# Two of the four weight sums of each FFN pair made by accumulating DMAs instead of VectorE

## The reference

```
h = rms_norm(x, ffn_norm_w)                                   # 256 x 2048
a = silu(h @ w_ffn_gate) * (h @ w_ffn_up)                     # both 2048 x 5632
x = x + a @ w_ffn_down                                        # 5632 x 2048
```

## Time and profile before

| | before |
|---|---|
| median of 3 runs | 2090.38 us (2086.85 to 2092.23) |
| the profiled execution | 2089.39 us |
| its span in the trace | 2087.7 us |
| TensorE busy | 2079.0 us |
| VectorE busy | 1372.1 us, 66% |
| ScalarE busy | 1072.2 us, 51% |
| GpSimd busy | 144.5 us, 7% |
| mean granted TensorE clock | 0.999 of full speed |

### The profile page before, as it was taken

How to read it: one execution, slowest core, us unless ns; L and a number is a source line. 1 busy time by engine, 2 the same in 40 slices (tenths; PEclk the granted TensorE clock), 3 DMA queues, 4 the chain that set the end, 5 groups by cost and what they waited for, 6 DMA issues and landing times.

```text
span 2087.7 us, 28374 instructions
## 1 busy us (share of the span) xinstructions
PE 2079.0 (100%) x9658; PEld 1715.0 (82%) x9658; DVE 1372.1 (66%) x1677; ACT 1072.2 (51%) x1380; POOL 144.5 (7%) x174
## 2 busy tenths in 40 slices
PE   9999999999999999999999999999999999999999
PEld 7888877778888888888888888888888888888887
DVE  6676456665767777777664555577777887764443
ACT  5444455554566666666654444455555555543333
POOL 1121000000012222222000000000000000000000
PEclk9999999999999999999999999999999999999999
DMA  7656665554565555555575555556656666566554
GB/s 237 205 177 209 197 198 169 163 176 138 189 204 172 189 186 185 183 182 181 171 231 193 191 189 187 189 176 197 201 161 198 205 199 202 161 223 205 199 200 141
DMA packets 207541, 394.46 MB, mean 189 GB/s; under 512 B 15665, under 2 KB 21218, under 8 KB 207218
## 3 DMA queue, kind: packets, MB, share of 16 engines
q1 hardware_dynamic: 204530, 384.79, 56.7%
q0 software_dynamic: 2336, 8.46, 1.3%
q10 hardware_dynamic: 608, 0.34, 0.1%
HBM read 387.18 MB, written 2.16 MB: 186 GB/s over the span
## 4 chain that ended last, share of the span: by engine, by line
PE 93%; DVE 3%; issue 2%; DMA 1%; ACT 1%; DVEq 0%; SPq 0%; ACTq 0%
PE acc L1500 84%; PE side L1516 3%; PE side L1870 2%; DVE w_raw L1311 1%; PE side L1743 1%; DVE w_lo L1306 1%; PE acc L1870 1%; PE side L1598 1%; ACT w_hi L784 1%; DMA w_raw<-in_w_in 0%; DMA x_row<-in_x 0%; PE side L1749 0%; PE acc L1516 0%; PE side L1672 0%; DVE w_lo L847 0%
## 5 line engine op out<-in xcount | busy, mean ns | idle before, releaser
L847 DVE TENSOR_TENSOR w_lo<-w_raw,w_hi 128x1024 fp32r<-128x1024 f32 x536 | 668.2, 1257 | 538.0 <-ACT w_hi L463 537.1
L463 ACT ACTIVATE w_hi<-w_raw 128x1024 fp32r<-128x1024 f32 x536 | 564.0, 1058 | 708.0 <-PE acc L1500 651.9
L1500 PE MATMUL acc<-w_hi,h_hi 128*128 128x512 f32 x1280 | 511.4, 400 | 0.1
L1500 PE MATMUL acc<-w_hi,h_lo 128*128 128x512 f32 x1280 | 499.9, 391 | 0.0
L1500 PE MATMUL acc<-w_lo,h_hi 128*128 128x512 f32 x1280 | 498.8, 390 | 0.0
L784 ACT ACTIVATE w_hi<-w_raw 128x1024 fp32r<-128x1024 f32 x209 | 220.2, 1060 | 211.5 <-PE acc L1500 120.9
L1306 DVE TENSOR_TENSOR w_lo<-w_raw,w_hi 128x1024 fp32r<-128x1024 f32 x209 | 252.6, 1223 | 96.1 <-ACT w_hi L784 89.9
L1500 PEld LDWEIGHTS acc<-w_hi,h_hi 128*128 128x128 f32 x1280 | 240.7, 188 | 52.5 <-issue 5.5
L1500 PEld LDWEIGHTS acc<-w_hi,h_lo 128*128 128x128 f32 x1280 | 240.5, 188 | 51.5
L1500 PEld LDWEIGHTS acc<-w_lo,h_hi 128*128 128x128 f32 x1280 | 241.0, 188 | 49.3 <-issue 1.9
L1500 PE MATMUL acc<-w_hi,x2T_hi 128*128 128x512 f32 x528 | 206.7, 391 | 0.1
(11 more groups left out here) (276 smaller groups left out, 2352.2 us busy)
## 6 DMA issues: line engine op xcount, KB each, us to landing
w_raw<-in_w_in SPq DMA_DIRECT2D x320, 512.0 KB, 4.2
w_raw<-in_w_ffn_gate SPq DMA_DIRECT2D x88, 512.0 KB, 3.7
w_raw<-in_w_ffn_up SPq DMA_DIRECT2D x88, 512.0 KB, 4.5
w_raw<-in_w_ffn_down SPq DMA_DIRECT2D x88, 512.0 KB, 3.5
w_raw<-in_w_ssm_proj SPq DMA_DIRECT2D x64, 512.0 KB, 4.2
w_raw<-in_w_attn_proj SPq DMA_DIRECT2D x32, 512.0 KB, 3.5
w_raw<-in_w_out SPq DMA_DIRECT2D x32, 512.0 KB, 3.5
acs_b<-acs_scratch POOLq DMA_DIRECT2D x16, 512.0 KB, 7.1
```

The source lines that it names most:

```text
L463: nc.scalar.activation(w_hi[:, r], w_raw[:, r], ACT.Copy).then_inc(hi_ready, 1)
L847: nc.vector.tensor_tensor(w_lo[:, r], w_raw[:, r], w_hi[:, r].bitcast(F32), ALU.subtract).then_inc(lo_ready, 1)
L1500: done = nc.tensor.matmul(acc[p][:, t], a[:, k0 + kk, cut], w[:, r, kk], start=first and kk == n == 0, stop=last and kk == UK - 1 and n == 2)
```

## The change

The first sum and the slot 1 sum are no longer VectorE instructions. GpSimd issues for each pair two DMAs that read one slot and add it to another in place. The first waits until the remainder of P1 is done (it overwrites slot 0) and slot 1 is loaded; the second waits until the first has landed (it overwrites slot 1, which the first reads) and slot 2 is loaded. Ahead of each DMA stands a multiply of two elements a partition on GpSimd. ScalarE's roundings of P5 and P7 wait for the DMAs' semaphores, and VectorE waits for the second DMA before the slot 2 sum, which keeps its place in VectorE's order.

```diff
+PLAIN_UNITS = UPC * (7 * D // CW + 2 * G) + 3 * UPC * D // CW
...
-        weights_summed, p1_ready, mids_free, gates_summed = (...)
+        first_summed, third_summed, weights_summed, p1_ready, mids_free, gates_summed = (...)
...
@@ scalar engine, operand_hi
                     if n < 3:
                         act.wait_ge(raw_in[source], raw.now(RAWS // 2) * (16 // RING) + 16)
+                    elif n == 4:
+                        act.wait_ge(third_summed, i * 16 + 16)
+                    elif n == 3:
+                        act.wait_ge(first_summed, i * 16 + 16)
                     else:
-                        act.wait_ge(weights_summed, i * 4 + (n - 2))
+                        act.wait_ge(weights_summed, i * 2 + (n - 4))
...
@@ vector engine, ffn_pair
-                    if at == FIRST7 - LEAD:
-
-                        dve.wait_ge(raw_in[1], raw.now(RAWS // 2) * (16 // RING) + 16)
-                        weights_sum(0, 0, 1)
                     if at == FIRST7 - LEAD + 2:
-                        weights_sum(1, 1, 2)
-                        dve.wait_ge(weights_summed, i * 4 + 2)
+
+                        dve.wait_ge(third_summed, i * 16 + 16)
                         weights_sum(2, 0, 2)
                     if at == FIRST7 - LEAD + 3:
-                        dve.wait_ge(weights_summed, i * 4 + 3)
+                        dve.wait_ge(weights_summed, i * 2 + 1)
                         weights_sum(3, 2, 3)
...
@@ gpsimd, behind everything it did before
+            def third_weights_sum(i):
+
+                pool.wait_ge(pool_step, own.now())
+                pool.wait_ge(lo_ready, i * OPERANDS + (PLAIN_UNITS + FIRST7 + 1))
+                pool.wait_ge(raw_in[1], i * (16 // RING * RAWS) + (16 // RING * (PLAIN_UNITS + RAWS // 2) + 16))
+                nc.gpsimd.tensor_tensor(y_scratch, y_ss, y_ss, ALU.mult).then_inc(pool_step, 1)
+                own.step()
+                pool.dma_start(w_raw[:, 0], w_raw[:, 1], accum_op=ALU.add).then_inc(first_summed, 16)
+                pool.wait_ge(pool_step, own.now())
+                pool.wait_ge(first_summed, i * 16 + 16)
+                pool.wait_ge(raw_in[2], i * (16 // RING * RAWS) + (16 // RING * (PLAIN_UNITS + RAWS // 2) + 16))
+                nc.gpsimd.tensor_tensor(y_scratch, y_ss, y_ss, ALU.mult).then_inc(pool_step, 1)
+                own.step()
+                pool.dma_start(w_raw[:, 1], w_raw[:, 2], accum_op=ALU.add).then_inc(third_summed, 16)
+
+            third_weights_sum(0)
+            with repeat(pool, FF // CW - 1, [(own, 2)]) as i:
+                third_weights_sum(i + 1)
```

More of the change, by code:

```diff
@@ L310, in layer @@
         s_summed, s_hi_ready, s_lo_ready = sem("s_summed"), sem("s_hi_ready"), sem("s_lo_ready")
-        weights_summed, p1_ready, mids_free, gates_summed = (sem(n) for n in ("weights_summed", "p1_ready", "mids_free", "gates_summed"))
+        first_summed, third_summed, weights_summed, p1_ready, mids_free, gates_summed = (sem(n) for n in ("first_summed", "third_summed", "weights_summed", "p1_ready", "mids_free", "gates_summed"))
         gate_f_ready, a_ready, a_T, a_hi_ready, a_lo_ready = (sem(n) for n in (
```

## The result

| | before | after |
|---|---|---|
| median | 2090.08 us | 2137.64 us |
| profiled execution's span | 2087.7 us | 2135.9 us |

The change makes the kernel slower: the ratio is 1.0229, 95% interval 1.0214 to 1.0243, 47.6 us. The forecast of 2168 us had the direction and the place; it was 30 us too high.

A forecast was written before the change was run, and what follows sets the result against it. TensorE was taken to bound the kernel. Delays of P5's remainder (68 us), the clock (9) and the first pair (2) added 79 us to 2089.4, giving 2168 us; own range 2146 to 2203, 8 in 10 within 2112 to 2245.

The forecast's parts named there:

- What bounds, and the most to be won: TensorE bounds; taking work from VectorE wins only TensorE's waits for remainders, 5.5 us in all 11 pairs.
- A delay of P5's remainder is one of TensorE, whole: At P5 in each pair, TensorE has no slack and loses the same time; forecast 6.2 us a pair, 68 us.
- The link: One of two chained steps per pair: GpSimd's wake-up, multiply and DMA; x = L + 0.35 us.
- L: Time from an accumulating DMA's issue to its landing, taken as 6.0 us; a pair's delay is 2L - 5.8 us.
- So I start from 4.2: Step sizing the landing from GpSimd's best 512 KB load, 4.2 us, as nothing else is in flight there.
- The surcharge for accumulating: Added to the plain landing: 1.44 us for reading 512 KB more, and something for the addition, reaching 6.0 us.
- the addition and second read cost almost nothing: Rival: landing 4.0 to 5 us, pairs 2.2 to 4.2 us later, kernel 2115 to 2146 us; chance 0.17.
- The clock: After TensorE's idle 5.4 us ahead of P5, lower clock loses 1.65 us, 0.8 uncovered a pair, 9 us in all.
- the rival of short landings: Rival with landings of 4.0 to 5 us, idle times too short for the clock to fall each time; chance 0.17.
- The slow accumulation: Rival: accumulating DMAs land in above 7.6 us; at 8.8 the kernel takes 2230 us; chance 0.23.
- the clock staying low for most of a pair: Rival: TensorE stays at 1.2 GHz for most of a pair; 2190 us and up; chance 0.03.
- Both DMAs hidden: Rival: landings below 2.9 us leave P5 ready early; at 2.6 the stall goes, 2084 us; chance 0.03.

The follow-up runs named there:

- c4_two_sums_out: The kernel before with the first and the slot 1 sum left out and no DMA in their place: 2083.74 us, ratio 0.9972.
- b1_copy: The changed kernel with both DMAs copying instead of adding: 2095.10 us, ratio 1.0032 to the kernel before.
- b2_half: The changed kernel with each accumulating DMA adding only the first 512 of its slot's 1024 columns: 2100.88 us, ratio 1.0059 to the kernel before.
- d1_together: The changed kernel with the first DMA adding slot 2 instead of slot 1, so both DMAs are in flight at once: 2105.48 us, ratio 1.0080 to before.
- c1_fill: The changed kernel with ten more matmuls a pair on TensorE ahead of P5, filling its idle time: 2129.28 us, ratio 1.0193 to the kernel before.
- e1_p5_ahead_fill: The changed kernel with the second DMA's wait and slot 2 sum behind P5's remainder, plus ten matmuls a pair ahead of P7: 2119.97 us, ratio 1.0146 to before.
- b3: The changed kernel with only the first sum made by a DMA, the slot 1 sum back on VectorE: 2091.67 us, ratio 1.0011 to before.
- b4: The changed kernel with only the slot 1 sum made by a DMA, the first sum back on VectorE: 2087.45 us, ratio 0.9994 to before.
- c3_p5_ahead: The changed kernel with VectorE's wait for the second DMA and the slot 2 sum moved behind P5's remainder: 2134.50 us, ratio 1.0223 to the kernel before.

## Why the prediction was right, and where it was off

**What bounds, and the most to be won: right.** VectorE matters to TensorE only in the train from P3 to P7; c4_two_sums_out, with both sums gone, wins 5.2 us where the earlier trace rows give 5.5.

**A delay of P5's remainder is one of TensorE, whole: right.** In the same pairs the delay by the rows (D less 6.55, times 11) and the time of the kernel above that of before, both in us:

| | landing | D | (D - 6.55) x 11 | measured |
|---|---|---|---|---|
| b1_copy | 2.9 | 6.65 | 1 | 5.9 |
| b2_half | 3.3 | 7.41 | 9 | 11.7 |
| d1_together | 4.6 and 6.4, at once | 7.83 | 14 | 16.6 |
| c1_fill | 4.5 | as after | 38 | 40.4 |
| after | 4.5 | 9.97 | 38 | 47.6 |

The excess of 2 to 5 us in the first four (10 in the last, with the lower clock) is the first pair, in which GpSimd is late. There D is 9.60, 9.85, 9.47, 12.91 and 12.86 us in the five kernels, 1.6 to 3.0 more than in their other pairs. With this the first four come to 4, 12, 16 and 41 us, all within 2 us of the measured times, and the last, with 8.4 us for the clock, to 49. In the kernel after, P1's remainder ends at 1380.48 and the sum starts at 1393.34: GpSimd is busy with the reciprocal square root until 1382.43, and its multiply then took 1.18 us instead of 0.18. I had put 2 us there and left the multiply out.

**The link: x = L + 0.35, measured 0.48.** 9.97 us for two links with 4.5 us each leave 0.48 a link. Between the first multiply and its DMA 0.24 us pass; my gap was too small. Over two links and 11 pairs this is 3 us, which the forecast had too low.

**The size of L: the term that was mis-sized.** I took 6.0, the DMAs took 4.5, which at 22 us for each us of L is 33 us. The miss is 30, as the link and the first pair took 3 and 1 us more than I had put. The step that failed is "So I start from 4.2". That was the best of GpSimd's loads from the scratch tensor in DRAM; a copy of the same size between two slots on quiet queues takes 2.9. Whether the place of the source or the traffic beside GpSimd's loads makes the difference, no run separates. The surcharge for accumulating was about right: I put 1.8 on top, b1_copy against the kernel after gives 1.6. So the result stands in the case that I called *the addition and second read cost almost nothing*, but for another reason: they cost 1.6 us, and the rest of a DMA is cheaper than I thought.

The Trainium skill (Collectives: The Full Stack, "The bandwidth ceiling: the fold count and why AG != RS != AR") says of a collective that the addition makes a transfer half as fast by its second source read. The runs agree for these DMAs inside one core: 202 GB/s for the accumulated bytes, 375 for the copied ones. The other page that I weighed, DMA: Bandwidth & Descriptors, "Anatomy of one DMA - SWDGE (gpsimd) path", was refused too quickly: its fit makes 3.2 us for a plain DMA of this size, an estimate, and the copy took 2.9.

**The clock: the size right, its condition wrong.** I put 0.8 us a pair and 9 us in all, c1_fill measured 0.84 and 7 to 8, and the cover by P7's lateness is real: the clock's full price is 1.58 us a pair by e1_p5_ahead_fill (1.65 put), of which 0.84 are left where P7 is late anyway. But I had these 9 us for idle times of 5.4 us, and said in the rival of short landings that such idle times would be too short for the clock to fall. They were 2.7 us, and it fell in every pair: the mean clock of each 47.8 us from the second pair to the tenth is 0.96. That the size came out right with the wrong idle time is luck.

**The rivals.** The slow accumulation and the clock staying low for most of a pair are out by the same rows. Both DMAs hidden would have needed D of 6.55 us, two landings of 2.8: the copies just miss it.

**What stays open.** Whether leaving out GpSimd's multiplies would shorten the links was not tried; by the rows of the fourth pair they and the gaps behind them take 0.64 us of D (1527.10 to 1527.52 and 1532.14 to 1532.36). The first small multiply took 1.18 us here, 1.0 to 1.3 us in six of the other kernels with a DMA, and 0.2 us in four; no run shows why.

## What to carry to other kernels

Price an engine that is "two thirds busy" by what the bounding engine loses to it, here 5.5 us in 2090, before giving its work to a DMA: a 1.2 us sum became 5 us of latency, harmless once a pair (b3, b4) and 3.4 us too long twice in a row. Look first at the order of the instructions in the late train: moving one sum behind one remainder gave the 0.2% that the best use of a DMA gave, though the rows account for less than half of it. And when a stall is added to a kernel that keeps TensorE at full clock, count the slower matmuls behind it as well, the more so where they have no other wait to hide in: 0.84 us a pair behind P5, 1.58 behind P7. Price a pair by the mean over the loop, not by one pair: single pairs of c1_fill take from 46.79 to 47.28 us.

## What was not expected of the hardware

- A DMA of 512 KB between two tiles on the chip, issued by GpSimd on quiet queues, lands in 2.9 us in every case but the first; accumulating in 4.5; accumulating 256 KB in 3.3. The bytes themselves take 1.4 us as a copy (375 GB/s) and 2.6 us accumulated (202 GB/s).
- GpSimd's issue of an accumulating DMA takes 0.87 us for 512 KB as for 256 KB, against 0.57 for a copy. Issued while another one was in flight it took 1.19 us (d1_together).
- Of two accumulating DMAs in flight at once, the first landed in 4.6 us, as if alone, and the second in 6.4.
- An idle time of 2.66 us of TensorE was enough for the granted clock to go to 1.2 GHz, about a microsecond after the matmuls had started again, in all ten pairs of the loop of the kernel after. In c3_p5_ahead the same idle time did so in nine of ten.
- The first small multiply of GpSimd behind its reciprocal square root took 1.18 us, all others of the kernel after 0.18 to 0.27.
